# A Fourier token-mixing layer: token transform first from the natural layout, scales on a half spectrum, weight blocks in another order

## What is computed

```python
sh1, sc1, g1, sh2, sc2, g2 = split(silu(c) @ w_ada[0] + b_ada[0], 6)   # other ones for the context
h = rms_norm(x, norm_gain[0, 0]) * (1 + sc1) + sh1
hg = h.reshape(256, 8, 128)                                            # tokens, groups, channels
y = fftn(hg, axes=(tokens, channels), norm='ortho').real
o = y.reshape(256, 1024) @ fnet_w_out + fnet_b_out
x = x + g1 * o
x = x + g2 * swiglu(rms_norm(x, norm_gain[0, 1]) * (1 + sc2) + sh2)
```

## Time and profile before

| | us |
|---|---|
| median of 3 runs | 1691.05 (1689.58 to 1691.51) |
| the profiled execution | 1692.76 |
| its span | 1690.9 |
| TensorE busy | 1527.1 (90%) |
| VectorE busy | 789.0 (47%) |
| ScalarE busy | 493.1 (29%) |
| GpSimd busy | 203.5 (12%) |
| granted TensorE clock, mean | 0.96 |

### The profile page before, as it was taken

The page is one execution under the profiler, slowest core; times in us unless marked ns, Lnnn a source line. Parts: engine busy times, 40 slices in busy tenths (PEclk is TensorE's granted clock), DMA queues, the critical chain, the costliest instruction groups (busy, mean ns, idle before and its releaser), DMA issues.

```text
span 1690.9 us, 20940 instructions
## 1 busy us (share of the span) xinstructions
PE 1527.1 (90%) x8522; PEld 1094.7 (65%) x8522; DVE 789.0 (47%) x1309; ACT 493.1 (29%) x989; POOL 203.5 (12%) x160
## 2 busy tenths in 40 slices
PE   5988999999999899979999897877899999999896
PEld 1666787877778599867999876766434434434333
DVE  2234776767644887656455557775302011110102
ACT  2222422222334445444444553632100000000001
POOL 0010111111011354001222111220000000000000
PEclk8999999999999899999999998988899999999998
DMA  9742354445322622116555455224499999999992
GB/s 391 275 174 75 144 186 187 181 174 199 137 87 87 275 107 93 51 50 238 211 176 189 148 190 221 100 100 174 196 427 426 427 427 426 427 426 427 427 426 113
DMA packets 53844, 388.64 MB, mean 230 GB/s; under 512 B 5984, under 2 KB 6128, under 8 KB 7152
## 3 DMA queue, kind: packets, MB, share of 16 engines
q1 hardware_dynamic: 53168, 384.18, 57.6%
q10 hardware_dynamic: 576, 3.06, 0.4%
HBM read 386.17 MB, written 1.05 MB: 229 GB/s over the span
## 4 chain that ended last, share of the span: by engine, by line
PE 74%; DMA 11%; DVE 10%; ACT 4%; issue 1%; DVEq 0%; SPq 0%; ACTq 0%; PEldq 0%
PE twin L658 44%; PE twin L1139 14%; DMA ring<-in_wblk 11%; PE twin L1195 3%; PE twin L646 2%; DVE wlo L1739 2%; PE twin L618 2%; PE twin L704 2%; ACT whi L1291 1%; PE twin L683 1%; PE twin L845 1%; PE twin L1129 1%; DVE rst L1787 1%; PE twin L869 1%; DVE Hl L1796 1%
## 5 line engine op out<-in xcount | busy, mean ns | idle before, releaser
L1739 DVE TENSOR_TENSOR wlo<-ring,whi 128x512 fp32r<-128x512 f32 (+1 forms) x306 | 274.4, 925 | 99.0 <-ACT whi L1291 97.2
L658 PE MATMUL twin<-Hh,whi 128*128 128x256 f32 (+1 forms) x864 | 287.4, 333 | 15.3 <-DVE Hl L1796 8.6
L658 PE MATMUL twin<-Hl,whi 128*128 128x256 f32 (+1 forms) x864 | 284.5, 329 | 0.0
L658 PE MATMUL twin<-Hh,wlo 128*128 128x256 f32 (+1 forms) x864 | 284.2, 329 | 0.0
L1291 ACT ACTIVATE whi<-ring 128x512 fp32r<-128x512 f32 (+1 forms) x408 | 224.9, 611 | 149.7 <-PE twin L658 149.7
L1642 POOL TENSOR_TENSOR wlo<-ring,whi 128x512 fp32r<-128x512 f32 x102 | 151.9, 1489 | 874.3 <-ACT whi L1291 874.3
L1139 PE MATMUL twin<-ring,xg 128*64 128x512 f32 x1024 | 227.8, 598 | 17.1 <-ACT xT L1604 8.2
L658 PEld LDWEIGHTS twin<-Hh,whi 128*128 128x128 f32 x864 | 166.6, 193 | 37.8 <-issue 11.7
L658 PE MATMUL twin<-hsp,whi 128*128 128x512 f32 (+1 forms) x704 | 178.2, 345 | 13.0 <-DVE hsp L1859 9.9
L1139 PEld LDWEIGHTS twin<-ring,xg 128*64 128x64 f32 x1024 | 76.1, 137 | 158.7 <-issue 146.3
L658 PEld LDWEIGHTS twin<-Hh,wlo 128*128 128x128 f32 x864 | 166.7, 193 | 14.1
(11 more groups left out here) (326 smaller groups left out, 1953.4 us busy)
## 6 DMA issues: line engine op xcount, KB each, us to landing
ring<-in_wblk SPq DMA_DIRECT2D x362, 1024.0 KB, 10.0
xT<-in_xin ACTq DMA_DIRECT2D x1, 2048.0 KB, 15.2
ring<-in_wblk SPq DMA_DIRECT2D x4, 512.0 KB, 3.7
out<-hTm SPq DMA_DIRECT2D x1, 1024.0 KB, 3.8
small<-in_small SPq DMA_DIRECT2D x1, 738.0 KB, 10.4
dft<-in_dft SPq DMA_DIRECT2D x1, 640.0 KB, 9.0
att<-in_rope ACTq DMA_DIRECT2D x1, 512.0 KB, 7.6
cons<-in_cons ACTq DMA_DIRECT2D x1, 296.0 KB, 8.3
```

The source lines that it names most:

```text
L658: t = e.matmul(out, a, b, start=start and n == 0, stop=stop and n == 2)
L1739: e.tensor_tensor(lo, w, hi.bitcast(F32), ALU.subtract).then_inc(*s_lov.up(m, h))
```

## The change

The transform over tokens comes first and takes x from a second copy in its natural layout, `xnat` (tokens on partitions, 4 tiles of 128 tokens by 1024 channels), so that it needs neither the modulation nor a normalised x. The root mean square of a token scales the row of the cosine and sine matrix instead (`fs`). As x is real, only half of the spectrum over tokens is computed: 127 sines and 129 cosines, 256 columns for each stream. The scale (1 + sc1) is a factor of a channel and is applied as the spectrum leaves PSUM into `Z`; the shift is constant over tokens and touches one column, frequency 0. Then the channel transform: one matmul of 258 columns with cosines and one of 254 with sines. ACT copies the sine part (`keep_sines`), DVE joins the halves (`join`): frequencies 1 to 127 are p - q, 129 to 255 are p + q read backwards. ACT makes the high part, POOL (no longer DVE) the low part. The first norm's `squares`, `sums`, `root` and `normed` are gone.

In the stream, 8 `ada` blocks come first, then `fnet` 0 and 1, the second 8 `ada` blocks, `fnet` 2 and 3, the third 8. Their matmuls stand behind output chunks 0, 1, 2 and 4, 5, 6 (`MODS`). Half of the FFN norm's sums stand behind chunk 6, and its squares follow each addition. `xT` is loaded by SP behind block 17. The `dft` constants shrink from 640 to 384 KB and are loaded by ACT; `small` and `wa2` come behind block 30.

```diff
-STREAM = [("ada", 0, s, k) for s in range(3) for k in range(8)]
+STREAM = [("ada", 0, 0, k) for k in range(8)]
...
+    if _t in (("fnet", 1), ("fnet", 3)):
+        STREAM += [("ada", 0, (_t[1] + 1) // 2, k) for k in range(8)]
...
 sync:
+            for t in range(4):
+                e.dma_start(xnat[:, t, :], xnat_d[:, t, :]).then_inc(s_tile[t], 16)
...
-                if n == 7:
-                    e.dma_start(dft[:, :], dft_d).then_inc(s_dft, 16)
+                if n == 17:
+                    e.dma_start(xT[:, :, :], xin_d).then_inc(s_x, 16)
+                if n == 30:
                     e.dma_start(small[:, :], small_d).then_inc(s_small, 16)
...
 pe:
+            def spectrum(c):
+                if c >= 6:
+                    if c % 2:
+                        e.wait_ge(*s_zv.at(c - 6))
                     else:
+                        e.wait_ge(*s_za.at(c - 6))
                 for s in range(2):
                     for t2 in range(2):
+                        if c == 0:
+                            e.wait_ge(*s_fs.at(2 * s + t2))
+                        t = e.matmul(bank[FIRST[c]][:, s * L:(s + 1) * L], xnat[:, 2 * s + t2, c * P:(c + 1) * P], fs[:, 2 * s + t2, :],
+                                     start=t2 == 0, stop=t2 == 1)
+                t.then_inc(*s_d1.up(c))
+            def channels(c):
+                e.wait_ge(*s_dc.at(c))
+                held = c + 2
+                if held < KC:
+                    if held % 2:
+                        e.wait_ge(*s_zv.at(held))
+                    else:
+                        e.wait_ge(*s_za.at(held))
+                else:
+                    e.wait_ge(*s_d2s.at(c - 6))
+                e.matmul(cosines(c), cd, Z[:, c, :, 127:256], start=True, stop=True)
+                e.matmul(sines(c), sd, Z[:, c, :, 0:127], start=True, stop=True).then_inc(*s_d2.up(c))
+            spectrum(0)
+            spectrum(1)
+            ada_rows(0, range(2))
+            spectrum(2)
+            spectrum(3)
+            ada_rows(0, range(2, 4))
+            spectrum(4)
+            spectrum(5)
+            ada_rows(0, range(4, 8))
+            e.wait_ge(s_cons, 16)
+            ada_cols(0)
+            spectrum(6)
+            spectrum(7)
+            for c in range(KC):
+                channels(c)
+            MODS = {0: (1, range(3)), 1: (1, range(3, 6)), 2: (1, range(6, 8)), 4: (2, range(2)), 5: (2, range(2, 5)), 6: (2, range(5, 8))}
+            for c in range(KC):
+                b, m = c // 2, c % 2
+                ws = parts(("fnet", b), KC)
+                if c == 0:
+                    e.wait_ge(*s_d2s.at(2))
+                if c >= 5:
+                    e.wait_ge(*s_fna.at(c - 5))
+                for k in range(KC):
+                    if c == 0:
+                        e.wait_ge(*s_d2l.at(k))
+                    t = mm3(fnet_bank(c)[:, :], [w[:, k, m * P:(m + 1) * P] for w in ws], [yh[:, k, :], yl[:, k, :]], k == 0, k == KC - 1)
+                t.then_inc(*s_wmm.up("fnet", b, m))
+                if c in MODS:
+                    ada_rows(*MODS[c])
+                if c == 3:
                     ada_cols(1)
+                if c == 6:
+                    sums(1, range(4))
             ada_cols(2)
+            sums(1, range(4, KC))
...
 act:
+            for t in range(4):
+                e.wait_ge(s_tile[t], 16)
+                e.activation(zflat[:, t * D:(t + 1) * D], xnat[:, t, :], ACT.Square, accum_out=xsq[:, t:t + 1]).then_inc(*s_xsum.up(t))
+            e.activation(xsq, xsq, ACT.Sqrt, bias=eps, scale=1.0 / D).then_inc(*s_xroot.up(0))
...
+            def keep_sines(c):
+                e.wait_ge(*s_d2.at(c))
+                if c >= 2:
+                    e.wait_ge(*s_d2s.at(c - 2))
+                e.activation(qsum[:, c % 2, :, :], sines(c), ACT.Copy).then_inc(*s_d2q.up(c))
+            def high_fnet(c):
+                e.wait_ge(*s_d2s.at(c))
+                e.activation(yh[:, c, :], fsum[:, c % 2, :, :].rearrange("p s n -> p (s n)"), ACT.Copy).then_inc(*s_d2h.up(c))
+            for c in range(KC):
+                if c % 2 == 0:
+                    e.wait_ge(*s_d1.at(c))
+                    for s in range(2):
+                        t = e.activation(Z[:, c, s, :], bank[FIRST[c]][:, s * L:(s + 1) * L], ACT.Copy, scale=NORM_A[0, s][:, c:c + 1])
+                    t.then_inc(*s_za.up(c))
+                if c >= 3:
+                    keep_sines(c - 3)
+                if c >= 4:
+                    high_fnet(c - 4)
+                if c == 6:
+                    split(4)
+            for c in range(5, KC):
+                keep_sines(c)
+                high_fnet(c - 1)
+            high_fnet(KC - 1)
             for c in range(KC):
                 if c % 2 == 0:
                     split(4 * (c // 2 + 2))
                 e.wait_ge(*s_wmm.at("fnet", c // 2, c % 2))
                 if c >= 4:
                     e.wait_ge(*s_fnx.at(c - 4, 1))
+                e.activation(tmp[:, c % 4, :], fnet_bank(c)[:, :], ACT.Identity, bias=col("fb", c)).then_inc(*s_fna.up(c))
+                if c == 2:
+                    arow_of(1)
+                if c == 6:
+                    arow_of(2)
+                if c >= 4:
+                    for a in {4: (0,), 5: (2,), 6: (), 7: (4, 6)}[c]:
+                        square(1, a, lambda a: e.wait_ge(*s_fnx.at(a, 1)))
...
 pool:
+            for c in range(KC):
+                e.wait_ge(*s_d2h.at(c))
+                e.tensor_tensor(yl[:, c, :], fsum[:, c % 2, :, :].rearrange("p s n -> p (s n)"), yh[:, c, :].bitcast(F32), ALU.subtract).then_inc(*s_d2l.up(c))
+                if c == 4:
+                    split(1)
             split(BLK["din", 0] + 1)
...
 dve:
+            e.reciprocal(xrec, xsq).then_inc(*own_v.up())
+            for t in range(4):
+                e.tensor_scalar(fs[:, t, :], fbase[:, t % 2, :], xrec[:, t:t + 1], None, ALU.mult).then_inc(*s_fs.up(t))
...
+            def join(c):
+                out, p, q = fsum[:, c % 2, :, :], cosines(c), qsum[:, c % 2, :, :]
+                e.wait_ge(*s_d2q.at(c))
+                if c >= 2:
+                    e.wait_ge(*s_d2l.at(c - 2))
+                e.tensor_copy(out[:, :, 0:129:128], p[:, :, 0:129:128])
+                e.tensor_tensor(out[:, :, 1:128], p[:, :, 1:128], q, ALU.subtract)
+                e.tensor_tensor(out[:, :, 129:256], p[:, :, 1:128][:, :, ::-1], q[:, :, ::-1], ALU.add).then_inc(*s_d2s.up(c))
+            for c in range(KC):
+                if c % 2:
+                    e.wait_ge(*s_d1.at(c))
+                    for s in range(2):
+                        t = e.tensor_scalar(Z[:, c, s, :], bank[FIRST[c]][:, s * L:(s + 1) * L], NORM_A[0, s][:, c:c + 1], None, ALU.mult)
+                    t.then_inc(*s_zv.up(c))
+                    e.wait_ge(*s_zv.at(c))
+                else:
+                    e.wait_ge(*s_za.at(c))
+                shift = mod[:, 0, :].rearrange("p (s x) -> p s x", s=2)[:, :, c:c + 1]
+                e.scalar_tensor_tensor(Z[:, c, :, 127:128], shift, math.sqrt(2.0), Z[:, c, :, 127:128], ALU.mult, ALU.add).then_inc(*s_dc.up(c))
+                if c >= 3:
+                    join(c - 3)
+                if c == 6:
+                    split(4)
+            for c in range(5, KC):
+                join(c)
+            split(8)
+            mods(1)
+            e.wait_ge(*s_mod.at(1, 1))
+            e.wait_ge(s_x, 16)
             for c in range(KC):
                 if c % 2 == 0:
                     split(4 * (c // 2 + 2))
...
                     e.scalar_tensor_tensor(xT[:, c, r], tmp[:, c % 4, r], modcol(0, s, 2, c), xT[:, c, r], ALU.mult, ALU.add).then_inc(*s_fnx.up(c, s))
+                if c % 2:
+                    square(1, c, lambda c: e.wait_ge(*s_fnx.at(c, 1)))
+            mods(2)
```

## The result

The changed kernel takes 1675.5 us (median of four runs, 1671.34 to 1677.36); the kernel before, run beside it, 1691.28 (1689.58 to 1693.95). The ratio is 0.9902, with a 95% interval from 0.9879 to 0.9925. It is faster by about 1%, as forecast, but 11.5 us slower than the 1664.0 forecast, and outside the range of 1656 to 1673. The profiled execution of the changed kernel took 1671.34 us, at a mean granted clock of 0.961.

A forecast was written before the change was run, and what follows sets the result against it. TensorE's path to the last sum of squares bounds the kernel: 50.9 us gained, less 14.9, 0.6, 9.0 and 3.4, plus 4.0, taken as 27.3 us earlier. Forecast 1664 us, range 1656 to 1673.

The forecast's parts named there:

- a hole at chunk 4: TensorE idle ahead of output chunk 4 for 5 to 8 us, ended by DVE's low part of weight block 2.
- Two of its signs: Expected in the profile after: output matmuls from 55 to 60 us, last sum at 133 to 139 us.
- Step 1: Start to first scales: TensorE starts at about 13.8, block 7 lands at 33.2, scales at 36.4 us.
- Step 2: Chain over eight channel groups: spectra 6 and 7 end at 40.9, POOL slowest, output matmuls begin at 57.7 us.
- the unknown prices: Costs outside the sum: dearer joins +5 to +9 us, half clock at 36 us +2, no group-chain half clock -1.
- Step 3: Output matmuls with modulation blocks between chunks: block 2 lands at 86.4, chunk 4 ends at 104.0, last sum at 135.8 us.
- The joins: DVE joining the spectrum's halves: backward operation taken at 0.41 us like the forward one, 1.0 us per join.
- (a): Dearer joins: backward reads or DVE's lock with POOL set the group chain; 1669 to 1673 us, chance 0.19.
- (c): Slower than before: the join's backward operation far off any row; 1700 us at 5 us each, chance 0.03.
- (d): Gain lost before the end: FFN's first four blocks come late, 10 us given back; 1674 us, chance 0.07.
- Rival (b): Cheaper middle: split and chunk 4 wait overlap, clock kept, 1656 to 1661, chance 0.16; against: early block 2 saves only 2.2.
- The last step: From span 1663.6 us to the median: 1.9 us around it, median 1.7 us under the profiled execution, giving 1664.

The follow-up runs named there:

- the earlier x: Changed kernel with x loaded behind block 11 instead of block 17: 1669.62 us, ratio 0.9881.
- the kernel with the late split: Changed kernel with DVE's split of weight block 0 behind its scaling of group 7 instead of ahead of it: 1674.38 us, ratio 0.9902.
- the changed kernel's second profile: Changed kernel run again without an edit: 1671.0 us over six runs, ratio 0.9892.
- the one with the old order: Changed kernel with all 24 modulation blocks first, x behind block 25, low parts ahead of DVE's wait for x: 1669.78 us, ratio 0.9858.

## Why the prediction was right and where it failed

**The shape** was right: output matmuls that begin when POOL's quarter of block 0 is done (it ended at 61.57, the matmuls began at 61.67, though the last channel matmul ended only 0.1 us before), a hole at chunk 4 that DVE's low part of block 2 ends (5.6 us of waiting for 5.7 forecast, and 1.4 for 2.2 ahead of the turning), half clock behind it (7.90 us for 7.4), joins cheap, the gain of the front passed whole to the end. Two of its signs didn't come: the output matmuls begin at 61.67 and not by 60, and the last sum ends at 142.61 and not by 139. The waits of TensorE from 40 to 142 us in the changed kernel (who waits, for whom, total, times, longest):

```profile
PE twin L687 <- DVE wlo L1804: 5.6, 1, 5.6
PE twin L716 <- DVE Z L1904: 4.8, 2, 4.0
```

**Step 1, to the first scales, late by 2.0 us.** TensorE starts at 14.19 (13.8). Block 7 is issued at 27.09 (26.8) but flies 7.86 us where I took 6.4 from between 4.9 alone and 9.9 behind another: it lands at 34.95, and spectrum 6 begins at 39.31 (37.3).

**Step 2, the priced-at-nothing half clock, 2.9 us.** Spectra 6 and 7 took 6.57 us, not 3.65. TensorE idled 1.6 us for block 7, 0.8 for the rows and 1.4 for the scales; from 38 to 40 us the clock was 0.57. I had the row that warned of it, and kept the case as "+2" among the unknown prices instead of in the sum. Keeping the engine busy removed it. In the other direction the group chain took 61.67 - 45.89 = 15.8 us where I had 16.8: POOL's low part took 1.27 us, not 1.52, and DVE's split 2.54, not 3.00. Together the output matmuls begin at 61.67, 4.0 us late.

**Step 3, another 2.8 us.** Block 2 was issued at 78.27 (73.3) and flew 13.66 us (13.1). So 4.0 of its 5.5 us of delay come from the start; some 0.7 from the chunks, of which the first took 5.96 us and the others 5.68 to 5.71 where I had 5.45 as a mean over 192 matmuls; 0.3 from small waits at the blocks between them; 0.6 from the flight. The sixth modulation block was late by 1.4 us, not 0.6, but block 2 is issued at the use of the fifth, so that isn't on this path. From its landing to chunk 4 took 10.0 us, as forecast (10.2). Chunk 4 adds 0.5 us and the later chunks 0.2 to 0.3 each, and the last sum is 6.8 us late.

**The joins.** The backward operation is the second of these rows, VectorE in order of time:

```profile
58.60 0.41 DVE L1896 TENSOR_TENSOR fsum<-twin,qsum 128x254 f32<-128x254 f32 x1
58.93 0.41 DVE L1897 TENSOR_TENSOR fsum<-twin,qsum 128x254 f32<-128x254 f32 x1
```

It costs what the forward one does. Rivals (a) and (c) are out. So is (d): the tail is 0.9 us shorter, not longer. Rival (b) as I wrote it didn't come either, but its counterargument was right, as the earlier x showed.

**The last step, from the profiled execution to the median, 5.9 us.** I took the 1.7 us by which the median of before lay under its profiled execution and subtracted it. After's median lies 4.2 us above its own. The profiled execution alone was late by 5.8 us (1671.34 for 1665.5) and would have been in the range. The runs of after go from a clock of 0.961 (1671.34 us) to 0.955 (1677.36), 1 us for 0.001 of clock, so the spread goes with half-clock phases that differ between executions of the same code. Two profiles show where. Here is a window of the kernel with the late split, whose 1532.0 us behind the last sum are 7.4 more than in the changed kernel's second profile with the same code:

```profile
760.00:780.00 20.00, 16.73 (x104) 8.57 (x103) 12.13 (x26) 8.72 (x19) 1.26 (x1) 0.83 0.96 385
```

and that second profile:

```profile
760.00:780.00 20.00, 16.47 (x123) 9.46 (x122) 12.51 (x26) 9.22 (x19) 1.30 (x1) 1.00 0.97 390
```

Up to 768 us the two run 0.3 us apart; at 788 it is 2.6 us. Another 1.2 us are added by 954 and some 3 by 1117. Between these, one and the same piece of the chain, in the second profile and in the kernel with the late split, is

```profile
1088.74 5.97 PE twin L687 x48
```

```profile
1093.94 7.46 PE twin L687 x48
```

at a clock of 1.00 and of 0.83 in the 20 us from 1080 on. Behind 1117 the distance stays at about 7 us.

So two terms of the sum failed, each by nearly 6 us, and either alone would have left the time inside the range. One is the front: the last sum came 6.8 us late, 0.9 of which the stretch behind it gave back, and its largest single error is the half clock over spectra 6 and 7, put at nothing and measured at 2.9 us. The other is to carry one difference of a profile and a median over to another kernel, as if it were a constant: taken as 1.7 us less, measured as 4.2 us more, and 1.9 us more in the six runs of the changed kernel's second time. Over eleven runs the changed kernel's median is 1671.5, so perhaps 4 of the 11.5 us are the luck of the first four; by the ratios, 0.9902 and then 0.9892, it is under 2. What makes a phase longer in one execution than in the next stays open. A deeper ring, which would bring the landings forward, wasn't tried.

**DVE and POOL.** VectorE and GpSimd in order of time in the changed kernel:

```profile
50.88 0.57 DVE L1910 SCALAR_TENSOR_TENSOR Z<-mod,Z 128x2 f32<-128x2 f32 x1
...
64.96 3.67 DVE L1804 TENSOR_TENSOR wlo<-ring,whi 128x512 fp32r<-128x512 f32 x3 [1.22 <-ACT whi L1323]
...
50.16 1.27 POOL L1706 TENSOR_TENSOR yl<-fsum,yh 128x512 fp32r<-128x512 f32 x1
```

The first row is an operation on two elements per partition with both inputs in SBUF. Alone it takes 0.16 us; here it takes 0.57 and ends at 51.45, when POOL's ends (51.43). The joins, with one input in PSUM, stay at 0.41 beside the same POOL operation. Three quarters of a split take 1.82 us alone (at 100.05, chain of waits of after), 2.54 with a POOL operation ending among them (at 52.55), and 3.67 beside a busy POOL at 64.96. The Trainium skill (SBUF — State Buffer, section SBUF: two separate sides) says that a VectorE operation with two SBUF inputs and a GpSimd operation that reads SBUF exclude each other for a whole instruction; the trace agrees. The price was not the one I put on it: the split of block 0 that the start waits for lost 0.7 us to POOL (2.54 for 1.82), and the 3.00 us that I took from before for a free DVE already held such a wait, for in that kernel a POOL operation of 1.56 us began at 123.62, right behind the split's start at 123.33.

## What to carry to other kernels

Before moving work to where an engine starts earlier, find the next landing or queue that holds the path and price the whole way to it: here an output stage that began 22 us earlier ended 1.5 to 3.2 us later than the one with the old order, because blocks and a wait had been put between its chunks. In an in-order queue, put work whose input is there (the split) ahead of a wait for something late (the modulation); this was worth 7 us, where data landing 7 us sooner gave 1, and an engine kept at full clock 2 to 3. Price each idle phase of TensorE with the half clock behind it inside the sum, and give the step from a profiled execution to a median a width of its own: here it went from 1.7 us down to 4.2 us up. And when one profile stands for a kernel, compare the piece that the edit changes, not only where the stage ends: the late split looked like 3 us at the start of the output matmuls and was worth 1.5.

## What the hardware showed that I had not expected

The half-clock phase behind the same idle time (1.4 us for the scales, behind waits of 1.3 to 1.6 us for block 7 and 0.8 us for the rows) isn't the same from one execution to the next: the same 16 records of spectra 6 and 7 took 5.15, 5.25, 5.35, 5.41, 6.57, 6.62 and 6.70 us, and 3.72 when the engine was kept busy ahead of them. Even the first 16 records of the program took 5.48 to 6.73. Reading PSUM backwards with VectorE, 254 fp32 elements, costs nothing over reading forwards (0.41 us both). And in the changed kernel three quarters of a split cost VectorE anything between 1.82 and 3.67 us, by what GpSimd does beside it.
